# Where a fused attention divides by its sums: in the probabilities, or in the gate

## What is computed

```python
logit = einsum('hqd,hkd->hqk', qc, k) * scale - slopes[:, None, None] * dist
logit = where(dist >= 0, logit, NEG_INF)
p = softmax(logit, axis=-1)
out = einsum('hqk,hkd->hqd', p, v)
...
moba_out = out * silu(a_z)
```

## Time and profile before

| | us |
|---|---|
| median of three runs (1857.81 to 1866.19) | 1863.85 |
| the profiled execution, its own time | 1863.21 |
| its span in the profile | 1861.5 |
| TensorE busy | 1809.1 |
| VectorE busy | 1489.4 |
| GpSimd busy | 1046.0 |
| ScalarE busy | 721.8 |

### The profile page before, as it was taken

The page is one execution under the profiler, slowest core; times in us unless marked ns, Lnnn a source line. Parts: engine busy times, 40 slices in busy tenths (PEclk is TensorE's granted clock), DMA queues, the critical chain, the costliest instruction groups (busy, mean ns, idle before and its releaser), DMA issues.

```text
span 1861.5 us, 29156 instructions
## 1 busy us (share of the span) xinstructions
PE 1809.1 (97%) x10491; PEld 1581.0 (85%) x10491; DVE 1489.4 (80%) x2485; ACT 721.8 (39%) x1166; POOL 1046.0 (56%) x651
## 2 busy tenths in 40 slices
PE   8999999999999999999999999999999999999987
PEld 6788778999999999999888888888888686887766
DVE  4886799869998888888489999999999796655542
ACT  2353333333333444444333333333333433326652
POOL 1342445788888555556567767676775463345012
PEclk8999999999999999999999999999999999999999
DMA  9542433799998689989899999999997232210011
GB/s 372 190 170 68 166 96 122 264 321 315 330 313 317 223 312 315 301 309 319 323 341 360 361 357 361 353 362 355 366 354 268 68 101 69 75 51 3 2 68 46
DMA packets 159934, 440.50 MB, mean 237 GB/s; under 512 B 13664, under 2 KB 62944, under 8 KB 156768
## 3 DMA queue, kind: packets, MB, share of 16 engines
q1 hardware_dynamic: 64416, 254.71, 39.3%
q0 software_dynamic: 36864, 134.23, 19.2%
q10 hardware_dynamic: 58560, 50.34, 8.2%
HBM read 386.80 MB, written 52.43 MB: 236 GB/s over the span
## 4 chain that ended last, share of the span: by engine, by line
PE 90%; DVE 5%; ACT 2%; issue 1%; DMA 1%; POOL 0%; SPq 0%; ACTq 0%; DVEq 0%; POOLq 0%
PE PS L972 15%; PE PS L981 15%; PE PS L973 15%; PE PS L1273 9%; PE PS L1274 9%; PE PS L1282 9%; PE PS L1240 5%; PE PS L1318 2%; PE PS L999 2%; PE PS L1309 1%; PE PS L1012 1%; DVE arena L1944 1%; PE PS L1460 1%; DMA gates_d<-arena 1%; PE PS L1198 1%
## 5 line engine op out<-in xcount | busy, mean ns | idle before, releaser
L860 POOL TENSOR_TENSOR w_lo<-raw,w_hi 128x1024 fp32r<-128x1024 f32 x299 | 720.2, 2409 | 702.5 <-ACT w_hi L1501 701.4
L1501 ACT ACTIVATE w_hi<-raw 128x1024 fp32r<-128x1024 f32 x332 | 352.0, 1060 | 926.1 <-PE PS L981 575.9
L972 PE MATMUL PS<-act_hi,w_hi 128*128 128x384 f32 (+1 forms) x1584 | 577.9, 365 | 2.2 <-DVE act_lo L1912 0.7
L973 PE MATMUL PS<-act_lo,w_hi 128*128 128x384 f32 (+1 forms) x1584 | 563.4, 356 | 0.0
L981 PE MATMUL PS<-act_hi,w_lo 128*128 128x384 f32 (+1 forms) x1584 | 337.1, 354 | 0.0
L972 PEld LDWEIGHTS PS<-act_hi,w_hi 128*128 128x128 f32 x1584 | 299.8, 189 | 34.8 <-DVE act_lo L2368 4.9
L973 PEld LDWEIGHTS PS<-act_lo,w_hi 128*128 128x128 f32 x1584 | 299.7, 189 | 23.0 <-issue 2.6
L1273 PE MATMUL PS<-w_hi,act_hi 128*128 128x512 f32 x768 | 300.4, 391 | 3.4 <-ACT arena L1657 3.4
L981 PEld LDWEIGHTS PS<-act_hi,w_lo 128*128 128x128 f32 x1584 | 284.5, 188 | 22.4 <-issue 0.5
L1274 PE MATMUL PS<-w_hi,act_lo 128*128 128x512 f32 x768 | 300.2, 391 | 0.0
L2315 DVE TENSOR_TENSOR act_lo<-arena,act_hi 128x384 fp32r<-128x384 f32 x128 | 249.1, 1946 | 29.7 <-ACT act_hi L1715 29.7
(11 more groups left out here) (355 smaller groups left out, 1929.7 us busy)
## 6 DMA issues: line engine op xcount, KB each, us to landing
raw<-in_expert_u SPq DMA_DIRECT2D x128, 512.0 KB, 5.5
raw<-in_expert_v SPq DMA_DIRECT2D x128, 512.0 KB, 5.9
raw<-in_w_in SPq DMA_DIRECT2D x52, 512.0 KB, 3.6
arena<-in_w_ada SPq DMA_DIRECT2D x24, 1024.0 KB, 9.4
gel_d<-arena ACTq DMA_DIRECT2D x64, 384.0 KB
gates_d<-arena ACTq DMA_DIRECT2D x12, 2048.0 KB, 15.2
arena<-gates_d SPq DMA_DIRECT2D x32, 768.0 KB, 7.0
arena<-gel_d SPq DMA_DIRECT2D x32, 768.0 KB, 9.1
```

The costliest lines, as they stand in the source:

```text
L860: pool.tensor_tensor(w_lo[:, k % SPLIT, :], raw[:, k % RAW, :], w_hi[:, k % SPLIT, :].bitcast(F32), ALU.subtract).then_inc(lo_split, 1)
L972: pe.matmul(own, w, act_hi[:, c, 0:n_tok], start=(i == 0), stop=False)
L973: pe.matmul(own, w, act_lo[:, c, 0:n_tok], start=False, stop=False)
L1501: act.activation(w_hi[:, k % SPLIT, :], raw[:, k % RAW, :], ACT.Copy).then_inc(hi_split, 1)
```

## The change

The exponentials stay unscaled, and so does their product with the values. The step `probs` has no part on any engine any more. Instead, one step `prow` follows the last `probs` of a head pair: VectorE inverts the eight columns of sums of the pair at once, and TensorE makes eight products, each with one column of inverses spread over 64 weight columns, against the identity; so every column of a bank holds the inverse of its query, for head 0 in the lower 64 partitions and for head 1 in the upper. The bank is a new job `pr` in the rotation of four. A step `pscale`, put behind the next `X`, `solve`, `tokens` or `scan` step (or ahead of `pv` or `gturn`), multiplies the gate by that bank, and the pair's result is then multiplied by the scaled gate.

```diff
@@ second_block_steps
         if 1 <= i <= MH * TB:
             steps.append(("probs", i - 1))
+            if i % 8 == 0:
+                steps.append(("prow", i // 8 - 1))
...
+    for m in range(MH // 2):
+        at = steps.index(("prow", m)) + 1
+        while steps[at][0] not in ("X", "solve", "tokens", "scan", "pv", "gturn"):
+            at += 1
+        steps.insert(at + 1 if steps[at][0] not in ("pv", "gturn") else at, ("pscale", m))
     return steps
@@ _jobs
+        if kind == "prow":
+            job(("pr", *n))
@@ emptied
-                    "av": (avt_ready, n + 1), "gt": (gn_done, n + 1)}[kind]
+                    "av": (avt_ready, n + 1), "gt": (gn_done, n + 1), "pr": (gate_scaled, n + 1)}[kind]
@@ TensorE
                 if kind == "turn":
-                    pe.wait_ge(p_ready, n + 1)
+                    pe.wait_ge(e_ready, n + 1)
...
+                if kind == "prow":
+                    pe.wait_ge(r_ready, n + 1)
+                    wait_free(pe, "pr", n)
+                    for q in range(TB):
+                        for e in range(2):
+                            k = 8 * n + 2 * q + e
+                            mm = pe.matmul(PS[64 * e:64 * e + 64, bank("pr", n), q * P:(q + 1) * P],
+                                           prec[:, k:k + 1].to_broadcast([P, 64]), ident[:, :], start=True, stop=True)
+                    full(mm, "pr", n)
@@ ScalarE
-                if kind == "probs":
-                    w = (n // 2 % 4 + 1) * P
-                    act.wait_ge(r_ready, n + 1)
-                    act.activation(L[:, n % 3, 0:w], L[:, n % 3, 0:w], ACT.Copy, scale=prec[:, n:n + 1]).then_inc(p_ready, 1)
@@ VectorE
-                if kind == "probs":
-                    dve.wait_ge(e_ready, n + 1)
-                    v.reciprocal(prec[:, n:n + 1], psum_[:, n:n + 1]).then_inc(r_ready, 1)
+                if kind == "pscale":
+                    if n == 0:
+                        dve.wait_ge(z_done, 8)
+                    wait_full(dve, "pr", n)
+                    v.scalar_tensor_tensor(out=az[:, n, :], in0=PS[:, bank("pr", n), :], scalar=0.5, in1=az[:, n, :],
+                                           op0=ALU.mult, op1=ALU.mult).then_inc(gate_scaled, 1)
+                if kind == "prow":
+                    dve.wait_ge(e_ready, 8 * n + 8)
+                    v.reciprocal(prec[:, 8 * n:8 * n + 8], psum_[:, 8 * n:8 * n + 8]).then_inc(r_ready, 1)
                 if kind == "pv" and n % 8 == 7:
                     m = n // 8
+                    if m:
+                        dve.wait_ge(alo_ready, 32 + m)
+                    dve.wait_ge(gate_scaled, m + 1)
                     dve.wait_ge(pv_done, n + 1)
-                    if m == 0:
-                        dve.wait_ge(z_done, 8)
-                    else:
-                        dve.wait_ge(alo_ready, 32 + m)
-                    v.scalar_tensor_tensor(out=tmp[:, m % 2, :], in0=PS[:, 0, :], scalar=0.5, in1=az[:, m, :],
-                                           op0=ALU.mult, op1=ALU.mult).then_inc(tmp_ready, 1)
+                    v.tensor_tensor(tmp[:, m % 2, :], PS[:, 0, :], az[:, m, :], ALU.mult).then_inc(tmp_ready, 1)
```

More of the change, by code:

```diff
@@ L543, in build @@
         e_ready = sem("e_ready")
-        p_ready = sem("p_ready")
+        gate_scaled = sem("gate_scaled")
         pt_ready = sem("pt_ready")
```

## The result

The changed kernel took **1873.11 us**, median of six runs (1867.98 to 1876.11), against 1862.08 us for the kernel before in six runs beside it: a ratio of 1.0053, 95% interval 1.0037 to 1.0070, so 7 to 13 us slower. The forecast was 1871 us, within a range of 1863 to 1879 us. Measured again (experiment 8), the ratio was 1.0042, interval 1.0027 to 1.0056. The two together lie about on the 0.5% that the prediction put between "no change" and "slower".

What follows compares the result with a forecast made beforehand. TensorE's own instruction stream was taken to set the time in 43 us of the attention; 2.7 + 2.7 + 0.5 + 2.0 = 7.9 us on a profiled 1863.2 us gave 1871 us, range 1863 to 1879 us.

Steps and rivals of the forecast that it cites:

- slower: Whole kernel: outcome slower by over 0.5%, above 1873.2 us; chance 0.28.
- pair 0: First head pair, full TensorE stretch: 0.5 us wait, 1.05 us products, 1.1 us wait, together 2.7 us.
- pair 1: Second head pair, one and a half levels later: same pattern of waits and products, again 2.7 us.
- pair 2, less 0.6 for the table load: Third head pair: 0.5 us later, bounds 0 and 1.6; the square root's table load about 0.6 us sooner.
- pair 3, from the table load on: Last head pair, serial tail: end 2.0 us later, with the table load 0.6 us sooner; bounds 1 and 3.0 us.
- Both waits: First two head pairs: TensorE waits 0.5 us for the reciprocal, then 1.1 us for the gate's multiplication.
- so this hand-over moves by nothing: Third head pair: ScalarE, without two 0.61 us copies, is free at 1757.2, so its copy near 1758.4 is not delayed.
- What is removed: ScalarE's 32 scaling copies, 17.7 us busy, and VectorE's 32 reciprocals: gain 1.8 us at most.
- ScalarE's relief decides: Rival, attention stage: earlier ScalarE evictions remove 6.4 us of TensorE waits, products stay hidden; 1857 us, chance 0.09.
- The tail: Last head pair: inverse waits behind 16 scalings, products take 1.97 us at lower clock; end 2.0 us later.
- The rival of the clock: Rival, first two pairs and tail: new waits each drop TensorE's clock, some 1.6 us each; 1876 us, chance 0.18.
- within 0.5%: Whole kernel: outcome within 0.5% (9.3 us), not told from no change; chance 0.67.

Runs made afterwards that it cites:

- experiment 8: The changed kernel measured once more, unchanged: 1871.49 us, ratio 1.0042 to the kernel before.
- run 7: The kernel before, with the transposes of the recurrence's output put behind the attention's last four steps on TensorE: ratio 1.0010 to the kernel before.
- experiment 1: The changed kernel with the gate's multiplication one step earlier on VectorE, ahead of the subtractions of block 1: ratio 1.0033 to the kernel before.
- experiment 4: The kernel before without the 32 scaling copies and 32 reciprocals, nothing in their place, so the division is left out: ratio 0.9982 to the kernel before.
- experiment 3: The changed kernel with the last head pair's reciprocal ahead of the 16 scalings of the recurrence's output on VectorE: ratio 1.0036 to the kernel before.
- experiment 5: The changed kernel with the gate's multiplication ahead of block 1's subtractions and all four wider reciprocals earlier on VectorE: ratio 1.0014 to the kernel before.
- 9: The kernel of experiment 5, with inverse products, gate's and output's multiplications of the first three pairs moved to TensorE's gap, output copy and low part later: ratio 0.9993.
- 11: The kernel before, with the output's multiplication, ScalarE copy and low part of the first three head pairs put off: ratio 1.0008 to the kernel before.

## Why the prediction was right, and where it was off

The time fell inside the range, 2 us above the forecast, by the mechanism forecast. That it came so near is in part luck: the forecast added 7.9 us to a profiled execution of 1863.2 us, while the runs beside the changed kernel put the kernel before at 1862.08 us and the change at 9.9 us (ratio 1.0053), or 7.8 us (1.0042). By terms, from the table, after against before:

| term | forecast | measured | from |
|---|---|---|---|
| pair 0 | 2.7 | 3.03 | B |
| pair 1 | 2.7 | 2.97 at equal clock | C, after less run 7 |
| pair 2, less 0.6 for the table load | -0.1 | 0.39 | D |
| pair 3, from the table load on | 2.6 | 2.71 and 1.32 | tail, after and run 8 |
| sum | 7.9 | 9.1 and 7.7 | |

- *Pairs 0 and 1.* Both waits stood where they were said to, and experiment 1 took the second away by moving one step. Over half of the missing 0.3 us is what a wait costs beyond its length: the group behind it takes 0.68 us, where 16 records of the running stream took a quarter of 2.01 us, 0.50 us.
- *Pair 2* is the term that was mis-sized: 0.5 us forecast, 1.0 us measured (0.39 us in D, and the 0.6 us of the table load, which came as forecast: from the last score product to the load it takes 5.63 us before and 5.02 us after). The step that failed: "so this hand-over moves by nothing", and the eviction behind it by 0.5 us. The prediction let ScalarE, freed of two copies, take up most of the wait and the products. ScalarE's eviction, first before, then after:

```profile
1760.22 0.57 ACT L1863 ACTIVATE arena<-PS 128x512 f32<-128x512 f32 x1
```

```profile
1762.29 0.60 ACT L1877 ACTIVATE arena<-PS 128x512 f32<-128x512 f32 x1 [0.32 <-PE PS L1469]
```

Counted from the start of D it came 0.68 us later, and the hand-over itself 0.30 us. The rest was lost further on. In experiment 4, without copies and without products, the second score product of D comes 0.90 us earlier than before, but the fourth only 0.48 us: between the second and the third its chain runs through VectorE and ScalarE, where that of before runs on TensorE. ScalarE's row there:

```profile
1763.79 1.14 ACT L1815 ACTIVATE arena<-PS,small 128x128 f32<-128x128 f32 x4 [1.89 <-DVE raw L2387]
```

So a freed ScalarE takes up 0.48 us of wait and products, where the forecast had 1.1 us (1.6 - 0.5). Against experiment 4 the change costs 27.36 - 25.88 = 1.48 us in D, nearly the whole of 0.5 + 1.09.
- *What is removed*: forecast 1.8 us at most, measured 1.09 us in the stage (experiment 4), 0.61 us at the table load and 0.48 us before it, none of it in the full stretches. That part of the rival "ScalarE's relief decides" is refuted.
- *The tail.* The reciprocal behind the scalings was the cause (experiment 3), and 1.97 us for the products was exact. How long the clock stays low behind them differs from run to run: 1.4 us between after and run 8.
- *The rival of the clock* asked for falls at the new waits. There were none: 1.00 in both stretches above, in spite of pauses of 0.49 and 1.15 us. The falls that came in other runs were in A, where nothing had changed, in C near 1738 us, where before had one too, and in the tail. The Trainium skill, TensorE: Matmul & The Clock Gate, section HAM oscillation, describes a kernel whose long waits between bursts of matmuls put the array back to half rate, so that the next burst starts there. The tail agrees, where TensorE had idled 5.35 us and the sixteen records took 1.97 instead of 1.09 us. Waits as short as the two new ones are not the section's case.
- *The chances.* 0.67 lay on "within 0.5%" and 0.28 on "slower". With 1.0053 and 1.0042 the truth is near that bound, and the profile cannot place it better: the terms' sum is 7.7 or 9.1 us depending on the tail's clock.

## What to carry to other kernels

Work taken from an engine that the chain does not pass through gives nothing back, while a microsecond put into a stream that is full costs a microsecond, and a wait there costs a little more than itself. When new work is woven into fixed streams, look first at where its producer and its consumer stand in the queue of the other engine: here two moved steps were worth 5 to 7 us (1.0042 and 1.0053 against 1.0014). Gaps in TensorE's stream hid some 1.5 us of the 2.6 us left in B and C (experiment 5 against before); 0.69 and 0.38 us stayed (9 against 11). What the removed work seems to leave free is worth only what the next limit behind it allows: here 0.48 us of 1.2 us of copies.

## What was not expected of the hardware

The granted clock falls to the lower level in some executions of a program and not in others. The clearest place is the beginning of part A, where nothing was changed: TensorE waits 1.43 to 1.44 us there in every kernel, and in nine of the fourteen profiles the clock then stands at 0.50 for some 3.5 us, in five it does not. The changed kernel's two profiles differ there. TensorE's rows in order of time, first after, then run 8:

```profile
1678.41 0.63 PE L1345 MATMUL PS<-ident,arena 128*128 128x128 f32 x4 [1.43 <-DVE arena L2528]
...
1679.39 3.18 PE L1327 MATMUL PS<-arena 64*64 64x64 f32 x80
```

```profile
1679.88 0.63 PE L1345 MATMUL PS<-ident,arena 128*128 128x128 f32 x4 [1.44 <-DVE arena L2528]
...
1680.86 4.08 PE L1327 MATMUL PS<-arena 64*64 64x64 f32 x80
```

The same 80 records take 0.9 us more. With the falls near 1738 us and in the tail this moves one profile by 1 to 6 us, against 8 to 10 us for the change itself, so single parts had to be compared and not spans. Why one execution falls and the next does not stays open.
